# A 1-core layer kernel: the first recurrent tile's preparation placed among the projection's last outputs, the first tile of mixed rows requested one stage earlier

## The reference

```
h    = modulate(rms_norm(x), shift1, scale1)          # both rows from c @ ada_w
proj = h @ w_in
y1   = rwkv7_time_mix(proj[..., :RWKV_COLS])          # 8 heads of 64, a recurrence over tokens
y2   = dsa_mix(q, ckv, q_idx, k_idx, w_idx)           # each token attends to 256 selected tokens
x    = x + (1 + gate1) * (concat(y1, y2) @ w_out)
h    = modulate(rms_norm(x), shift2, scale2)
x    = x + (1 + gate2) * hierarchical_moe(h)          # 32 experts, 2 of one group of 8 for each token
out  = modulate(rms_norm(x), shift_f, scale_f)
```

## Time and profile before

| | |
|---|---|
| runs | 2021.02, 2019.51, 2021.01 us; median 2021.01 |
| the profiled execution | 2025.51 us, its span 2023.9 us |
| busy: PE, DVE, ACT, POOL | 1627.5, 868.5, 605.5, 397.7 us |
| stages by the trace (us from the span's start) | project to 425, mix 428 to 1091, route 1095 to 1299, experts and finish to 2024 |
| mean DMA rate | 179 GB/s; over 300 GB/s in most slices of the experts stage |

### The profile page before, as it was taken

The page is one execution under the profiler, slowest core; times in us unless marked ns, Lnnn a source line. Parts: engine busy times, 40 slices in busy tenths (PEclk is TensorE's granted clock), DMA queues, the critical chain, the costliest instruction groups (busy, mean ns, idle before and its releaser), DMA issues. The chain is left out here.

```text
span 2023.9 us, 40655 instructions
## 1 busy us (share of the span) xinstructions
PE 1627.5 (80%) x16134; PEld 1082.5 (53%) x16135; DVE 868.5 (43%) x1904; ACT 605.5 (30%) x1169; POOL 397.7 (20%) x825
## 2 busy tenths in 40 slices
PE   3999999857778778787886996387889997999920
PEld 2744444337666666666664454355656665666610
DVE  2257686346666666757652222221112221222228
ACT  3214887613323433433331222011111111111112
POOL 7321467511110110101100000011111111111123
PEclk8899999978888989999997997598989998999965
DMA  9493434320111100000002555399999999999855
GB/s 309 163 376 137 169 118 154 117 73 26 35 45 55 36 12 25 13 24 17 7 7 84 179 211 183 112 327 370 377 360 336 332 348 342 362 339 333 259 192 189
DMA packets 195984, 362.09 MB, mean 179 GB/s; under 512 B 29984, under 2 KB 67920, under 8 KB 195856
## 3 DMA queue, kind: packets, MB, share of 16 engines
q1 hardware_dynamic: 158128, 305.98, 44.0%
q0 software_dynamic: 37728, 54.34, 8.8%
HBM read 303.48 MB, written 56.64 MB: 178 GB/s over the span
## 5 line engine op out<-in xcount | busy, mean ns | idle before, releaser
L1834 PE MATMUL psX<-arena 128*64 128x256 f32 x1536 | 193.7, 410 | 48.1 <-DMA arena<-in_e_down_dram 46.5
L1834 PEld LDWEIGHTS psX<-arena 128*64 128x64 f32 x1536 | 123.4, 148 | 131.8 <-issue 85.3
L1858 PE MATMUL psP<-arena 128*64 128x512 f32 x768 | 175.4, 598 | 0.0
L1796 DVE SCALAR_TENSOR_TENSOR arena<-arena,psX 128x256 f32<-128x256 f32 x48 | 20.2, 421 | 346.8 <-ACT arena L1767 341.0
L792 PE MATMUL psX<-arena 128*128 128x512 f32 x320 | 142.6, 601 | 3.4 <-DVE arena L693 1.9
L487 ACT ACTIVATE arena<-arena 128x1024 bf16<-128x1024 f32 (+5 forms) x138 | 134.2, 973 | 32.5 <-POOL arena L444 28.6
L792 PE MATMUL psP<-arena 128*128 128x512 f32 x320 | 141.2, 595 | 2.9 <-DVE arena L693 2.9
L1771 ACT ACTIVATE arena<-psP 128x512 f32<-128x512 f32 x48 | 28.7, 597 | 378.9 <-PE psP L1858 378.9
L1745 POOL DMA_DIRECT2D expert_rows<-arena x48 | 41.7, 869 | 496.5 <-ACT arena L1771 467.6
L889 POOL TENSOR_TENSOR st<-st,mhalf 128x8 f32<-128x8 f32 x16 | 26.7, 1670 | 559.2 <-DVE st L1105 427.9
L1639 PE MATMUL psP<-arena 128*128 128x512 f32 x256 | 116.4, 614 | 16.1 <-DMA arena<-mix_T 10.9
(11 more groups left out here) (399 smaller groups left out, 2806.3 us busy)
## 6 DMA issues: line engine op xcount, KB each, us to landing
arena<-in_e_gate_dram SPq DMA_DIRECT2D x32, 2048.0 KB
arena<-in_e_up_dram SPq DMA_DIRECT2D x32, 2048.0 KB
arena<-in_e_down_dram SPq DMA_DIRECT2D x32, 2048.0 KB, 25.2
arena<-in_ada_w_dram SPq DMA_DIRECT2D x12, 2048.0 KB, 15.1
expert_rows<-Z POOLq DMA_DIRECT2D x34, 512.0 KB, 17.6
expert_rows<-arena POOLq DMA_DIRECT2D x48, 256.0 KB
proj_T<-arena SPq DMA_DIRECT2D x36, 256.0 KB, 2.0
arena<-in_x_dram SPq DMA_DIRECT2D x16, 512.0 KB, 10.4
```

The lines of the kernel that those rows point to most:

```text
L1796: dve.scalar_tensor_tensor(out=hid, in0=hid, scalar=1.0, in1=psum["X0"][:, 0:DE // 2], op0=ALU.add, op1=ALU.mult).then_inc(q("half_gated"), 1)
L1834: mm = pe.matmul(psum["X0"][BLK * h:BLK * h + BLK, 0:DE // 2], xT[:, k, :], gate_w[u][:, k, DE // 2 * h:DE // 2 * (h + 1)], start=(k == 0) ...
L1858: mm = pe.matmul(psum["P0"][BLK * half:BLK * half + BLK, :], hidT[:, f, h, :], down_w[u][:, KE // 2 * h + f, D // 2 * half:D // 2 * (half ...
```

## The change

It does five things.

1. Within a group of weight columns the outputs now run through all first halves and then all second halves. In the last group (8 outputs, 32 to 39) the first halves are outputs 32 to 35. `carry` gets four columns, one for each column tile of a group. The modulation vectors come after outputs 5, 10, 15, 20, 25, 30; DVE takes its pieces ahead of `modulation` and no longer behind it.
2. After output 35 SP waits for the stores of outputs 32 to 35 and loads the first tile of the mix stage into `pm_first`. The preparation of tile 0 leaves the mix stage. It is cut in three turns, which PE, ACT and DVE each run behind their part of outputs 37, 38 and 39. POOL does its part (`memset` of `dx`, `kkr`, the power) behind its search.
3. The gate rows of tile 0 (one matmul and one copy) stay at the start of the mix stage as `rows_of_gate(0)`.
4. In the mix stage SP, ahead of the stores of tile 6, waits for the end of the last preparation and for the stores of tile 0, and loads tile 0's mixed rows (`next_mix`) to where the route stage wants them. The route stage loads and awaits rows only from tile 1 on.
5. `EARLY_K` is 5: one block of `wout` (0.5 MB) more is loaded in the route stage. The memory plan is rearranged for all this.

The core of the diff:

```diff
@@ constants, order of the outputs @@
-EARLY_K = 6
+EARLY_K = 5
...
+            first_after = (37, 38, 39)
-            outs = [(g, ct, half) for g, (_, _, tiles) in enumerate(W_GROUPS) for ct in tiles for half in range(2)]
+            outs = [(g, ct, half) for g, (_, _, tiles) in enumerate(W_GROUPS) for half in range(2) for ct in tiles]
...
-            vector_after = {6: 2, 12: 3, 18: 4, 24: 5, 30: 6, 36: 7}
+            vector_after = {5: 2, 10: 3, 15: 4, 20: 5, 25: 6, 30: 7}
...
@@ SP, in its loop over the outputs @@
+                    if i == 35:
+                        sp.wait_ge(*at("projected", i))
+                        for n in range(4):
+                            sp.wait_ge(*at(f"stored{n}", i - 3 + n))
+                        sp.dma_start(pm_first, p_d[0:NRW, :, 0:P].rearrange("c p s -> p c s")).then_inc(*sig("first_mixed", 0, by=16))
...
@@ POOL, behind its search @@
+                pool.wait_ge(*at("first_mixed", 0))
+                link(pool, pool.memset(dx, 1.0), "edge_one", 0)
+                link(pool, pool.tensor_tensor(g4(kkr), pm_first[:, 4:8, :], over(c_kk, P), ALU.mult), "kkr", 0)
+                pool.wait_ge(*at("kk_var", 0))
+                link(pool, pool.tensor_tensor(s_kk[:, 8:16], s_kk[:, 0:8], mhalf[:, 0:8], ALU.pow), "kk_rs", 0)
...
@@ ACT @@
+                def first_tile():
+                    act.wait_ge(*at("first_mixed", 0))
+                    link(act, act.activation(lo[0:64, :], pm_first[0:64, 12, :], ACT.Tanh), "first_step", 0)
+                    link(act, act.activation(lo[64:128, :], pm_first[64:128, 12, :], ACT.Copy), "first_step", 1)
+                    link(act, act.activation(gsig, pm_first[:, 13, :], ACT.Tanh, scale=0.5), "lora_in", 0)
+                    act.wait_ge(*at("kkr", 0))
+                    link(act, act.activation(rnb, kkr, ACT.Square), "kk_sq", 0)
+                    yield
+                    act.wait_ge(*at("offsets_halved", 0))
+                    act.wait_ge(*at("lora_done", 0))
+                    for p in range(NPAIR):
+                        link(act, act.activation(g4(sgd)[:, p, :], g4(psum["T0"])[:, p, :], ACT.Tanh, scale=0.5, bias=c_w0[:, p:p + 1]), "dec_tanh", p)
+                    for p in range(NPAIR):
+                        link(act, act.activation(g4(av)[:, p, :], g4(psum["T1"])[:, p, :], ACT.Tanh, scale=0.5, bias=c_a0[:, p:p + 1]), "aaa_tanh", p)
+                    yield
+                    act.wait_ge(*at("cum", 0))
+                    act.wait_ge(*at("edge_one", 0))
+                    link(act, act.activation(dx[:, :, 1:CHUNK + 1], cum.rearrange("p (a b) -> p a b", b=CHUNK), ACT.Exp, scale=-DECAY), "first_step", 2)
+                    link(act, act.activation(invE, cum, ACT.Exp, scale=DECAY), "decays", 0)
+                    act.wait_ge(*at("v_turned", 0))
+                    link(act, act.activation(V[:, 0].rearrange("p q g i -> p (q g i)"), psum["T0"], ACT.Copy), "v_rows", 0)
+                    yield
...
@@ DVE @@
+                def first_tile():
+                    dve.wait_ge(*at("lora_in", 0))
+                    link(dve, dve.tensor_scalar(gsig, gsig, 0.5, 0.5, ALU.mult, ALU.add), "g_sig", 0)
+                    dve.wait_ge(*at("kk_ss", 0))
+                    link(dve, dve.tensor_scalar(s_kk[:, 0:8], psum["W1"][:, 0:8], 1e-24, None, ALU.max), "kk_var", 0)
+                    yield
+                    dve.wait_ge(*at("dec_tanh", NPAIR - 1))
+                    step(dve.tensor_scalar(sgd, sgd, 0.5, 0.5, ALU.mult, ALU.add))
+                    link(dve, dve.tensor_tensor_scan(cum, scan_reset[:, :], sgd, 0.0, ALU.mult, ALU.add), "cum", 0)
+                    dve.wait_ge(*at("aaa_tanh", NPAIR - 1))
+                    step(dve.tensor_scalar(av, av, 0.5, 0.5, ALU.mult, ALU.add))
+                    dve.wait_ge(*at("kk_rs", 0))
+                    link(dve, dve.tensor_copy(g8(rnb), over(s_kk[:, 8:16], HEAD)), "kk_rs_wide", 0)
+                    step(dve.scalar_tensor_tensor(out=g4(kmod), in0=g4(av), scalar=-1.0, in1=over(c_ka, P), op0=ALU.add, op1=ALU.mult))
+                    step(dve.scalar_tensor_tensor(out=g4(kmod), in0=g4(kmod), scalar=1.0, in1=pm_first[:, 4:8, :], op0=ALU.add, op1=ALU.mult))
+                    step(dve.tensor_tensor(g4(sgd), pm_first[:, 0:4, :], g4(kmod), ALU.mult))
+                    link(dve, dve.tensor_tensor(g4(sgd), g4(sgd), over(c_rk, P), ALU.mult), "bonus", 0)
+                    yield
+                    dve.wait_ge(*at("kk_spread", 0))
+                    link(dve, dve.tensor_tensor(kkr, kkr, psum["T1"], ALU.mult), "kk", 0)
+                    dve.wait_ge(*at("bonus_done", 0))
+                    link(dve, dve.tensor_copy(s_bon[0], psum["W1"][:, 0:8]), "bonus_rows", 0)
+                    yield
...
                 for i, (g, ct, half) in enumerate(outs):
                     if ct < NRW:
                         shift(i)
+                    for _ in range(pieces_after(i)):
+                        pick(i)
                     if i in vector_after:
                         modulation(vector_after[i])
-                    for _ in range(pieces_after(i)):
-                        pick(i)
+                    if i in first_after:
+                        next(first_turns)
                 for k in range(len(SELECT)):
...
@@ PE @@
+                def first_tile():
+                    pe.wait_ge(*at("lora_in", 0))
+                    fill(pe, "T0", "dec_tanh", NPAIR - 1)
+                    fill(pe, "T1", "aaa_tanh", NPAIR - 1)
+                    for p in range(NPAIR):
+                        for g in range(2):
+                            mm = pe.matmul(g4(psum[f"T{g}"])[:, p, :], wlora[part(g), P * p:P * p + P], lo[part(g), :], start=True, stop=True)
+                    mm.then_inc(*sig("lora_done", 0))
+                    pe.wait_ge(*at("kk_sq", 0))
+                    fill(pe, "W1", "kk_var", 0)
+                    for p in range(NPAIR):
+                        mm = pe.matmul(psum["W1"][:, 2 * p:2 * p + 2], g4(rnb)[:, p, :], blk2[:, :], start=True, stop=True)
+                    mm.then_inc(*sig("kk_ss", 0))
+                    yield
+                    fill(pe, "T0", "v_rows", 0)
+                    for p in range(NPAIR):
+                        mm = pe.transpose(g4(psum["T0"])[:, p, :], pm_first[:, 8 + p, :], ident[:, :])
+                    mm.then_inc(*sig("v_turned", 0))
+                    pe.wait_ge(*at("kk_rs_wide", 0))
+                    fill(pe, "T1", "kk", 0)
+                    for p in range(NPAIR):
+                        mm = pe.matmul(g4(psum["T1"])[:, p, :], g4(rnb)[:, p, :], ident[:, :], start=True, stop=True)
+                    mm.then_inc(*sig("kk_spread", 0))
+                    yield
+                    pe.wait_ge(*at("bonus", 0))
+                    fill(pe, "W1", "bonus_rows", 0)
+                    for p in range(NPAIR):
+                        mm = pe.matmul(psum["W1"][:, 2 * p:2 * p + 2], g4(sgd)[:, p, :], blk2[:, :], start=True, stop=True)
+                    mm.then_inc(*sig("bonus_done", 0))
+                    yield
...
@@ mix stage, SP @@
+                    if t == NT - 1:
+                        sp.wait_ge(*at("g_done", NT - 1))
+                        sp.wait_ge(*at("kk_spread", NT - 1))
+                        sp.wait_ge(*at("dsa_stored", 0))
+                        sp.wait_ge(*at("rwkv_stored", 0))
+                        sp.dma_start(next_mix, mix_d[:, :, tile(0)].rearrange("c p s -> p c s")).then_inc(*sig("next_mix", 0, by=16))
...
@@ mix stage, PE and ACT @@
-                for _ in prepare(0):
-                    pass
+                rows_of_gate(0)
...
@@ route stage, SP @@
                 def load(t):
                     if t >= 2:
                         sp.wait_ge(*at("out_done", t - 2))
-                    sp.dma_start(kt(mixT, t), mix_d[:, :, tile(t)].rearrange("c p s -> p c s")).then_inc(*sig(f"mix_loaded{t % 2}", t, by=16))
+                    if t:
+                        sp.dma_start(kt(mixT, t), mix_d[:, :, tile(t)].rearrange("c p s -> p c s")).then_inc(*sig(f"mix_loaded{t % 2}", t, by=16))
...
@@ route stage, PE @@
                 def project_out(t):
-                    pe.wait_ge(*at(f"mix_loaded{t % 2}", t))
+                    if t:
+                        pe.wait_ge(*at(f"mix_loaded{t % 2}", t))
```

More of the change, by code:

```diff
@@ L226, in sparse_attention_moe_layer @@
         smask = [masks.take(P * (t + 1) // 2).bitcast(BF16) for t in SELECT]
+        both = Arena(arena_t, ARENA)
+        both.at = KD * D
+        rnb, lo, gsig = both.take(RW), both.take(P), both.take(P)
+        both.take(2 * P)
+        pm_first, kkr, sgd, av, kmod, cum = both.take(NRW, P), *(both.take(RW) for _ in range(5))
+        dx, invE, V = both.take(NH, CHUNK + 1), both.take(RW), both.take(2, NPAIR, 2, CHUNK)
+        next_mix = arena_t[:, KD * D:KD * D + D].rearrange("p (k s) -> p k s", k=KD)
+        s_kk, s_bon = st[:, 72:88], (st[:, 24:32], st[:, 32:40])
         with ExitStack() as scope:
```

(5 more changed lines are left out.)

62 lines of the change are left out of this document (30 added, 32 removed).

## The result

The change makes the kernel slower: 2032.44 us median of 10 runs (2025.86 to 2040.15) against 2022.13 us (10 runs, 2015.81 to 2027.38); the ratio is 1.0052, with a 95% interval from 1.0037 to 1.0066, so 7.5 to 13.3 us. The profiled execution took 2032.45 us, its span is 2030.8. I had forecast 2.5 us less than before and not more than 2023.5.

A forecast was written before the change was run, and what follows sets the result against it. A chain of small dependent steps bounds the project stage's end; PE waits for mixed rows at route's start. +2.0 us at the first place and -4.5 in route gave -2.5, from 2021.0 to 2018.5; range 2012.5 to 2023.5.

The forecast's parts named there:

- Output 35: Project stage: earlier modulation vectors let DVE finish this output 0.9 us earlier than 411.9, bounds 0 and 3.
- Store to request: End of project stage: SP requests the first tile 2.2 us after output 35 is finished.
- transfer: End of project stage: loading the first tile alone takes 5.1 us, so it is there at 419.2.
- The first stop: Behind output 37, PE stands some 13 us until ACT has the tile, with outputs 38 and 39 queued behind.
- First turn: Preparation behind output 37: from the tile's arrival, ACT's three steps and PE's two groups take 4.9 us.
- second stop: Between outputs 38 and 39: emptying, tanh's, DVE's steps and PE's spreading take 7.0 us, output 39 queued behind.
- Clock: Outputs 38 and 39, each behind a stop, pay 1.5 and 2.0 us for half clock, 3.5 together, bounds 0 and 6.
- The mix stage: SP's new waits ahead of tile 6's stores and the 0.5 MB transfer inside this stage cost nothing.
- Route: Start of the route stage: PE starts 6.45 us earlier, then waits for `wout`; -4.5 us, bounds -6.7 and 0.
- (a): Rival: the stops cost no clock and the search gains its 3 us; -8.5 us, 2012.5; chance 0.24.
- (b): Rival: `wout` lands last, route gives between 0 and -1.7, total about +1, 2022; chance 0.13.
- (c): Rival: half clock kept through outputs 38 and 39, each 13.7 us instead of 6.9; about +8, 2029; chance 0.11.

The follow-up runs named there:

- the early tile: The changed kernel with the first tile's load requested behind output 32 and reading input weights, so wrong numbers: 2020.84 us, ratio 0.9982.
- the late turns: The changed kernel with all three turns of the first tile's preparation behind output 39: 2016.55 us, ratio 0.9962.

## Why the prediction was wrong

I go through the sum step by step; tile 0 was to start at 454.0 + 3.5 - 0.9 = 456.6 and started at 467.8, 11.2 us later.

- **Output 35, forecast 0.9 us earlier, came 8.0 later: 8.9 of the 11.2.** This is the step that failed. I had costed the vectors by their own length and by DVE's and ACT's waits, and not by the bank that they are made in. My reason, "three outputs apart from these waits", looked at the waits that a vector ends and not at the one that it begins. The runs put it on the vectors' places: away from the units 9.9 us come back, in the kernel before the same places cost 5.5. The trace puts most of it on the one behind output 20 (PE's 4.07 us of wait and 1.7 of half clock, ACT's 5.85 us of standing), some of it on the one behind output 10 (1.30). Only 0.35 of the 8.0 lay ahead of PE's first output. My bounds (0 and 3 us of gain) had no loss in them, without a reason that excluded one. The gain itself is there once the vectors stand elsewhere: 2.0 us by output 32.
- **Store to request 2.7 us (2.2 forecast), transfer 5.6 (5.1).** 1.0 together.
- **The first stop: 13.88 us, forecast some 13.** Right, though its start lay 8.4 us later than forecast and its end 9. That the outputs are laid behind the wait was the heart of the argument, and the early tile and the late turns both confirm it.
- **First turn 4.8 (4.9), second stop 6.9 (7.0), end of output 39 to mix start 5.6 (5.5), start of the mix to PE's first matmul 3.8 (3.65).** Right.
- **Clock.** Output 38 took 10.07 us, 3.2 more than the 6.9 of full clock, where I took 1.5; output 39 took 8.36, 1.4 more, where I took 2.0. Together 4.6 instead of 3.5. Here the Trainium skill, "TensorE: Matmul & The Clock Gate", section "Why this matters for your kernels", advises against idle gaps between bursts of matmuls, because PE drops back to half rate. The rows agree for the first stop: behind 13.9 us output 38 paid 3.2, behind 1.65 us it paid nothing (7.11). Behind the second one, two waits of 2.28 and 1.98 us, output 39 paid 1.4.
- **The mix stage: nothing.** The trace has 2.7 us less there, which lies within what the table above shows for this stage (634 to 641).
- **Route: forecast -4.5, in the two traces -4.0 to DVE's first step and -4.2 to the experts.** The mechanism was right (start at the barrier, one stop at the eleventh matmul, 2.33 us). But the size stands on one profile of the kernel before, the longer of its two; between the means of the profiles it is 1.9 us, since the clock took back 1.3 of the 3.1 us at tile 1, where I had 0.5 for the clock in the whole stage. The times show nothing of it: without it the changed kernel is 0.4 us faster, it alone makes the kernel before 0.4 us slower, each within some 3 us. The last blocks of `wout` landed 9.8 us behind the first request of the stage (1115.31 less 1105.50; 9.7 to 9.9 in the nine profiles with this part), where order of issue had put them at 9.0 and the end of all transfers at 12.3. The Trainium skill, "DMA: Bandwidth & Descriptors", section "Two DMAs through the same engine are not ordered", allows the later end; this trace is nearer to the order of issue.

The sum by the trace is +13.2 - 2.7 - 4.2 = +6.3 and, with 0.9 more in the experts' stage, close to the 6.9 of the two spans; the medians have +10.3. The 3.4 us between these two are the distance of the profiled run of the kernel before (2025.51) from its median (2022.13); the changed kernel was profiled at its median.

Of the rivals, (a) had nothing for it; (b) did not come by its own road, `wout` not being last, though the route part was worth as little as it said; (c) came in part: 4.6 us of clock, not 13.7, since the clock rose again inside output 38 (0.50 over 433 to 437, 0.84 over 437 to 443). The time that (c) gave, 2029, was the nearest, and by luck: its reason was the wrong one. None of the rivals had a delay ahead of output 35, and the check that I named myself ("wrong if DVE finishes output 35 well ahead of 411") looked only to the other side.

What stays open: how much each of the five places costs by itself, since no run moves the vector behind output 20 alone; and why the clock fell at tile 1 of the route stage in each of the nine profiles with the route part.

## What to carry to other kernels

When work is moved on an engine with an order written out by hand, list for each new neighbour the memory banks that it takes over, and who last reads them: a piece that costs nothing by its length can wait for a slow reader. Moved work that waits for data must stand behind everything that doesn't need the data; here the same code, placed one or two outputs later, turned 10 us of loss into 8 us of gain. When two profiles are compared, count from a point that both share: 1.7 to 1.9 us of some differences here lay ahead of PE's first output. And before a gain of 4 us is forecast from one place of one profile, look at how far that place varies by itself: the same stage of the same kernel differed by 2.3 us between two profiles.

## What was not expected of the hardware

The half clock behind a short wait is not fixed by the code. Behind the same wait of 2.73 us, before tile 1 of the route stage, with the same matmuls after it, the granted clock stayed at 2.4 GHz throughout (16.7 us from residual to residual, 3 of 14 profiles), fell to 1.2 GHz for about 3 us (18.2 to 18.4, nine profiles) or for about 6 (19.7 and 19.8, two); the kernel before showed two of these in two profiles. It seems not to be free of the code either: all three profiles without a fall are of kernels that request tile 0's rows in the route stage. The wait of 13.9 to 14.8 us ahead of the first turn cost in every profile that has it: the small matmuls of the turn took 2.08 us instead of 1.16, and the output behind them 9.2 to 10.1 instead of 7.11.
